# A two-block float32 model on one NeuronCore: order of the first up-projection stage's vector steps, and of the first pair of weight units

## The reference

```
xn = rms_norm(h, g_ffn) * (1 + sc2) + sh2
up = causal_dwconv(xn @ w_up, conv_ffn_w, conv_ffn_b)      # width 3, 2 * 2816 channels
val, gte = split(up, 2)
h = h + ga2 * ((silu(gte) * val) @ w_down)
```

## Time and profile before

| what | value |
|---|---|
| median of 3 runs | 1910.57 us (1907.24 to 1911.62) |
| the profiled execution's own time | 1908.22 us |
| its span, first to last instruction | 1906.4 us |
| PE busy | 1801.7 us, 95% |
| POOL busy | 1445.2 us, 76% |
| DVE busy | 1054.7 us, 55% |
| ACT busy | 532.1 us, 28% |
| mean granted TensorE clock | 0.980 |

### The profile page before, as it was taken

How to read it: one execution, slowest core, us unless ns; L and a number is a source line. 1 busy time by engine, 2 the same in 40 slices (tenths; PEclk the granted TensorE clock), 3 DMA queues, 4 the chain that set the end, 5 groups by cost and what they waited for, 6 DMA issues and landing times.

```text
span 1906.4 us, 33520 instructions
## 1 busy us (share of the span) xinstructions
PE 1801.7 (95%) x11324; PEld 1585.4 (83%) x11324; DVE 1054.7 (55%) x1674; ACT 532.1 (28%) x784; POOL 1445.2 (76%) x2245
## 2 busy tenths in 40 slices
PE   4999988999898999999899999999999999999997
PEld 2767765578698999888799999999999999999885
DVE  6548887745746666621375556656555555555101
ACT  3236662310221111110244434443443221111000
POOL 1768982469978888799677767767776889999885
PEclk8999997999999999999999999999999999999999
DMA  8332332334522222233222222222222223323332
GB/s 311 116 111 88 94 105 100 100 133 154 152 80 88 77 88 77 88 99 99 66 79 78 67 68 77 78 67 68 77 68 69 86 88 99 94 93 91 102 105 88
DMA packets 54299, 184.42 MB, mean 97 GB/s; under 512 B 6673, under 2 KB 7857, under 8 KB 54226
## 3 DMA queue, kind: packets, MB, share of 16 engines
q1 hardware_dynamic: 48690, 169.20, 28.5%
q10 hardware_dynamic: 5536, 14.16, 2.2%
HBM read 178.62 MB, written 4.72 MB: 96 GB/s over the span
## 4 chain that ended last, share of the span: by engine, by line
PE 55%; POOL 14%; issue 11%; DVE 7%; DVEq 5%; ACT 3%; DMA 3%; SPq 1%; POOLq 0%; ACTq 0%
PE gp L378 17%; PE gp L379 17%; PE gp L380 17%; POOL Wlo L369 9%; POOL Whi L366 3%; PE A L680 3%; DMA raw<-units 2%; DVEq L1395 2%; POOL probe L365 2%; DVEq L1446 2%; DVE ffn_act L1402 1%; DVE ffn_gate L1399 1%; DVE AClo L1379 1%; DVE ffn_gate L1397 1%; ACT ffn_val L953 1%
## 5 line engine op out<-in xcount | busy, mean ns | idle before, releaser
L369 POOL TENSOR_TENSOR Wlo<-raw,Whi 128x256 fp32r<-128x256 f32 x1120 | 961.3, 879 | 46.8
L378 PE MATMUL gp<-XNhi,Whi 128*128 128x264 f32 (+3 forms) x2736 | 845.3, 309 | 57.2 <-DVE XNlo L1072 23.8
L379 PE MATMUL gp<-XNlo,Whi 128*128 128x264 f32 (+3 forms) x2736 | 834.5, 305 | 0.0
L380 PE MATMUL gp<-XNhi,Wlo 128*128 128x264 f32 (+3 forms) x2736 | 831.7, 304 | 0.0
L378 PEld LDWEIGHTS gp<-XNhi,Whi 128*128 128x128 f32 x2736 | 517.3, 189 | 89.8 <-POOL Wlo L369 33.2
L379 PEld LDWEIGHTS gp<-XNlo,Whi 128*128 128x128 f32 x2736 | 517.4, 189 | 25.5 <-issue 2.2
L380 PEld LDWEIGHTS gp<-XNhi,Wlo 128*128 128x128 f32 x2736 | 516.6, 189 | 22.9
L365 POOL TENSOR_TENSOR probe<-raw 1x1 f32<-1x1 f32 x560 | 164.5, 294 | 393.2 <-PE gp L380 350.6
L366 POOL TENSOR_SCALAR Whi<-raw 128x512 fp32r<-128x512 f32 x560 | 344.3, 615 | 0.0
L378 PE MATMUL gp<-AChi,Whi 128*128 128x512 f32 x352 | 139.1, 395 | 1.2 <-DVE ZZ L1394 1.2
L379 PE MATMUL gp<-AClo,Whi 128*128 128x512 f32 x352 | 139.0, 395 | 0.0
(11 more groups left out here) (301 smaller groups left out, 2230.7 us busy)
## 6 DMA issues: line engine op xcount, KB each, us to landing
raw<-units SPq DMA_DIRECT2D x280, 512.0 KB, 3.5
AW<-ada SPq DMA_DIRECT2D x16, 512.0 KB, 9.1
AWL<-ada SPq DMA_DIRECT2D x16, 512.0 KB, 4.0
AWL<-ada ACTq DMA_DIRECT2D x16, 512.0 KB, 4.2
bias_rows<-RB ACTq DMA_DIRECT2D x1, 2560.0 KB, 16.4
H<-xT SPq DMA_DIRECT2D x1, 2048.0 KB, 8.9
BIAS<-bias_rows ACTq DMA_DIRECT2D x1, 2048.0 KB, 9.3
out<-H SPq DMA_DIRECT2D x8, 256.0 KB, 2.1
```

What stands on the lines that cost most here:

```text
L369: ins = pool.tensor_tensor(lo[:, c:c + UNIT // 4], src[:, c:c + UNIT // 4], hi[:, c:c + UNIT // 4].bitcast(F32), ALU.subtract)
L378: pe.matmul(dst, Whi[s][:, k, :], rhi, start=start, stop=False)
L379: pe.matmul(dst, Whi[s][:, k, :], rlo, start=False, stop=False)
L380: return pe.matmul(dst, Wlo[s][:, k, :], rhi, start=False, stop=stop)
```

## The change

In first_pair the second unit stands six steps behind the first one (lag = 6) and stats(m) is called at step 6. So PE does chunks 0 to 5 of the first unit, the statistics, chunks 6 and 7 of the first unit by turns with 0 and 1 of the second, and then the other six of the second. This holds for all three first pairs.

In the first up stage DVE's order is changed: the product and the split of a pair are issued inside the steps of the next pair, the product in the place where DVE waited for ACT's first tap of the value, the split where it waited for that of the gate. For this the value has two buffers; gate, silu and product keep one each. ACT may run one pair further ahead of act_done, whose count starts one higher. The loops are unrolled by two.

```diff
-            YV, YG, SL, AF = [sb(f"ffn_{n}", [P, S], frame=f) for n in ("val", "gate", "silu", "act")]
+            YV, YV1, YG, SL, AF = [sb(f"ffn_{n}", [P, S], frame=f) for n in ("val", "val1", "gate", "silu", "act")]
+            YVS = (YV, YV1)
...
-                lag = 1
+                lag = 6
                 for j in range(KC + lag):
-                    if j == KC // 2 and midway is not None:
+                    if j == lag and midway is not None:
                         midway()
...
-            all_units(*down(U_DN, G_DN, (act_done, 1)))
+            all_units(*down(U_DN, G_DN, (act_done, 2)))
...
-            with act.Fori(0, FC) as i:
-                for c, (y, first) in enumerate(((YV, yv_first), (YG, yg_first))):
-                    act.wait_ge(z_ready, i * 2 + c + 1)
-                    if c == 0:
-                        act.wait_ge(act_done, i + 1)
...
+            with act.Fori(0, FC // 2) as i:
+                for j in range(2):
+                    for c, (y, first) in enumerate(((YVS[j], yv_first), (YG, yg_first))):
+                        act.wait_ge(z_ready, i * 4 + (j * 2 + c + 1))
+                        if c == 0:
+                            act.wait_ge(act_done, i * 2 + j + 1)
...
+            dve.memset(probe[0:1, 22:23], 0.0).then_inc(act_done, 1)
...
-            with dve.Fori(0, FC) as i:
...
+            def product_up(i, j):
+                dve.wait_ge(silu_ready, i * 2 + j + 1)
+                dve.tensor_tensor(AF[:, :], SL[:, :], YVS[j][:, :], ALU.mult)
+                dve.drain()
+
+            def pair_up(i, j, before):
...
                     dve.drain().then_inc(z_ready, 1)
-                    dve.wait_ge(first, i + 1)
+                    if before is not None:
+                        if c == 0:
+                            product_up(*before)
+                        else:
+                            split_act(before[0] * 2 + before[1], act_done)
+                    dve.wait_ge(first, i * 2 + j + 1)
                     dve.scalar_tensor_tensor(y[:, :], ZZ[:, c, 1:1 + S], fv(4 * c + 1), y[:, :], ALU.mult, ALU.add)
...
-                dve.wait_ge(silu_ready, i + 1)
-                dve.tensor_tensor(AF[:, :], SL[:, :], YV[:, :], ALU.mult)
-                split_act(i, act_done)
+            pair_up(0, 0, None)
+            pair_up(0, 1, (0, 0))
+            with dve.Fori(1, FC // 2) as i:
+                pair_up(i, 0, (i - 1, 1))
+                pair_up(i, 1, (i, 0))
+            product_up(FC // 2 - 1, 1)
+            split_act(FC - 1, act_done)
```

More of the change, by code:

```diff
@@ L947, in _ @@
             act.preload_act_table(ACT.Silu)
-            with act.Fori(0, FC) as i:
-                for c, (y, first) in enumerate(((YV, yv_first), (YG, yg_first))):
-                    act.wait_ge(z_ready, i * 2 + c + 1)
-                    if c == 0:
-                        act.wait_ge(act_done, i + 1)
[L953 to L956, removed]
+            with act.Fori(0, FC // 2) as i:
[4 more added lines that the diff above has]
+                            act.wait_ge(act_done, i * 2 + j + 1)
+                        act.activation(y[:, :], ZZ[:, c, 2:2 + S], ACT.Identity, bias=BC[:, c:c + 1],
+                                       scale=V[:, bass.ds(VEC["ffn"] + i * 16 + (j * 8 + 4 * c + 2), 1)]).then_inc(first, 1)
+                    act.wait_ge(yg_ready, i * 2 + j + 1)
+                    act.activation(SL[:, :], YG[:, :], ACT.Silu).then_inc(silu_ready, 1)
             norm_stats(2)
@@ L1384, in _ @@
             dve.wait_ge(rstd_ready, 2)
-            with dve.Fori(0, FC) as i:
-                def fv(c):
[L1387 to L1391, removed]
+            b0 = region(S + 2)
+            def product_up(i, j):
[3 more added lines that the diff above has]
+            def pair_up(i, j, before):
+                def fv(c):
+                    return V[:, bass.ds(VEC["ffn"] + i * 16 + (j * 8 + c), 1)]
+                taps = TAPS[:, bass.ds(i * 2 + j, 1), :].rearrange("p a c -> p (a c)")
+                for c, (y, first) in enumerate(((YVS[j], yv_first), (YG, yg_first))):
+                    dve.wait_ge(unit_done, U_UP + i * 4 + (j * 2 + c + 1 + 2))
                     dve.scalar_tensor_tensor(BC[:, c:c + 1], gp[c][:, b0 + 1:b0 + 2], taps[:, c:c + 1], fv(4 * c + 3), ALU.mult, ALU.add)
```

## The result

The changed kernel runs at a median of 1885.4 us (1883.61 to 1887.6, four runs) against 1911.09 before; the ratio is 0.9861 with a 95% interval of 0.9827 to 0.9895. That is 1.4% faster; the forecast was 1883 us. The profiled execution took 1887.12 us with a span of 1885.3.

A forecast was written before the change was run, and what follows sets the result against it. DVE, with its waits for ACT, was taken to bound the first up stage. 23.8 + 6.3 - 2.4 = 27.7 us off the profiled 1908.22 gave 1880.5; with the median 2.35 us above that execution, 1883 was named, range 1874 to 1897.

The forecast's parts named there:

- the loop: First up stage: interleaving takes pairs from 12.645 to 11.55 us, POOL a little over PE's pace; 23.8 us gained.
- Rival 1: First up stage's loop: PE alone paces it, POOL's price 0.27 or less; total 1878.5 us; chance 0.2.
- rival 2: First up stage's loop: POOL bounds it at 11.8 to 12.35 us a pair; total 1888 to 1899 us; chance 0.22.
- Two of my signs: Loop: PE's waits are for L369 if POOL binds; DVE has no wait over 0.2 us before L1397.
- The price of POOL: Loop: each us of DVE's busy time slows POOL by 0.30 us, with DVE at 8.28 us a pair.
- the third rival: Loop: each us of DVE's two-input work costs POOL a full us; 14.9 us a pair, total 1952; chance 0.02.
- The first up pair: First up stage's first pair: no gap between matmuls, end 13.3 us after its start, 6.3 us gained.
- The first projection: First projection's first pair: late activations and a later clock rise lose 2.4 us, range 0 to 3.0.
- The second up stage's first pair: Second up stage: PE has no gap, so the edit is worth 0; about 1 us lost if XN came late.
- DVE's last chain: End of first up stage: last split moves to about 10 us after the last up unit; no cost was added.

The follow-up runs named there:

- e4: Changed kernel, but POOL makes only the first 256 columns of Wlo in each half in the first up stage's units; loop 237.4 us, median 1886.1 us.
- e1: Kernel before plus the interleaving of DVE's steps alone, lag 1 and statistics at step 4; 1893.0 us, ratio 0.9892.
- e8b: Changed kernel plus one DVE tensor_tensor per unit of the first up stage, first input from PSUM, second from SBUF; 1887.0 us, ratio 0.9874.
- e8a: Changed kernel plus one DVE tensor_tensor per unit of the first up stage, both inputs from SBUF; loop 261.3 us, median 1903.2 us.
- e3: Changed kernel with lag 1 in the first projection alone; 1882.9 us, ratio 0.9852.
- e9: The changed kernel run again, unaltered, for its profile; 1881.5 us, ratio 0.9845.

## Why the prediction was right, and where it was not

**The total** (1883, measured 1885.4) and the loop came out by the stated mechanism. The wait for L1394 is gone. POOL took its place: I put 11.55 us a pair for the loop, measured are 11.52; 23.8 us of gain against 24.3. e4 shows that it is POOL, e1 that the interleaving alone gives 21.9 us of it. That the loop is met so closely is in part luck. Where POOL sets the pace a pair takes 11.65 us, which over 20 pairs would have been 21.8 us of gain by my own sum; and I gave POOL no lead, which keeps the first eight pairs at 11.31. The two errors nearly cancel. Rival 1 was short by POOL's 4.5 us, rival 2 needed 11.8 us a pair. Two of my signs did not show: no wait of a matmul for L369 is listed in the loop (they are too short), and DVE still waits 0.38 us ahead of the first tap of the value, not under 0.2.

**The price of POOL** was 0.30 us per us of DVE, and the profile gives (2.916 - 2.26) / 1.987 us of DVE per half = 0.33; DVE's busy time per pair came out at 7.9 instead of 8.28 us, so the product is nearly the same. Its unit did not survive e8b. By the Trainium skill (SBUF — State Buffer, "Who interferes with whom") an instruction of VectorE with at most one input from SBUF, outside its two-port modes, does not contend with GpSimd. e8b agrees: the loop took 241.4 us with such an instruction more in each unit, 241.9 without. The same section of the Trainium skill calls the ports that the two share an exclusive lock. e8a shows what that came to here: 0.43 us on POOL for each added instruction, which itself took 1.22 us, so the third rival's price of a full us per us was not seen.

**The first up pair** was to end 13.3 us after its start and did after 13.43; the gain is 6.2 us against 6.3. The root was ready early enough, and gp[0] too.

**The first projection** was the step that was sized too low: 2.4 us, with 3.0 as the upper end; the mean of the runs is 3.0 (21.2 against 18.2). The cause is the one given, a clock that rises later. In the changed kernel PE had six chunks with pauses of some 0.6 us between them while the activations came, then ran at the lower clock to 58.45 us, 5.7 us after its last pause, where I had put 4.7 (54.3 to 59.0 us):

```profile
52.74 0.79 PE L379 MATMUL gp<-XNhi,Whi 128*128 128x512 f32 x1 [0.59 <-DVE XNlo L1074]
...
58.03 0.63 PE L379 MATMUL gp<-XNhi,Whi 128*128 128x512 f32 x1
58.45 0.43 PE L380 MATMUL gp<-XNlo,Whi 128*128 128x512 f32 x1
58.72 0.39 PE L381 MATMUL gp<-XNhi,Wlo 128*128 128x512 f32 x1
```

P0 follows that moment. With lag 6 the matmuls became faster 14.6 (e4) to 17.1 us (changed) after the first one, and P0 took 20.6 to 21.8 us (in the mean 15.9 and 21.2; my 59.0 us was 15.6 after it); with lag 1, 9.4 (e1) to 12.3 us (e3) after it, and P0 took 17.5 to 18.8. I missed that POOL, released earlier, now works beside DVE's last activations: they are there 13.6 us after the first matmul in all six kernels with lag 6, and after 12.2 to 12.7 us in those with lag 1. PE had to wait for neither of the last two chunks.

**The second up stage's first pair** was put at 0; matmuls 9216 to 9408, which hold it, take 29.8 us with lag 6 in all kernels that have it and 29.5 with lag 1: 0.3 us lost.

**What I left out.** First, a POOL that bounds the loop has nothing in hand when the down stage begins. In the first hundred matmuls of that stage the changed kernel, e1, e3, e8b and e9 lose 0.6 us against before, e8a 0.9, and e4, with POOL's work cut, nothing. I had only asked whether DVE's last chain was in time for the down stage (it was). The rest of the 1.4 us by which the stretch behind is longer (141.1 against 139.7) falls at its other end, where PE, after a wait of 5.6 us for activations, runs at the lower clock for a stretch that differs between profiles. Second, the places where the clock falls outside the stage: the recurrence stage took 491.5 to 500.6 us, and five such places, of 1.5 us each, are most of the difference of 9. Added up for the profiled execution: -30.5 in the stage, +3.6 in P0 (this run's) and -2.0 since its activations came earlier, +1.4 behind the stage, and the remaining 6.4 us in stretches that the change does not touch, of which four more places of low clock (at 123, 345, 1410 and 1461 us, 1.5 us each) are the most.

## What to carry to other kernels

When an engine's wait for a helper is filled with the work of the pair before, ask at once who shares a resource with the work that now runs without pause. Here POOL was 15% idle, and one look at how its instructions lengthen beside DVE's put the new bound within 0.1 us a pair (11.55 against 11.65). Ask also how far ahead the helper is when the loop begins: here that was worth 2.4 us. Price such contention by kind of instruction: in this loop one with two inputs in SBUF cost the neighbour 0.43 us, one with an input from PSUM nothing; so look for the first kind. Taking a cast from SBUF to SBUF away from DVE helped too: one fewer per pair took 4 x 0.041 = 0.16 us off POOL's pair, all effects together, and 3.8 us off the stage. And a change of a shared helper, like the lag here, is to be priced at each place that calls it: with weights late a long lag pays, with activations late it costs.

Where stages outside the change differ by several us between runs of one kernel, compare the stage that was changed by the starts of its own first and last matmul; here that was good to 0.2 us (255.3 and 255.5), while the spans differed by 6.6.

## What the runs showed of the hardware

- PE's clock fell to its lower level in the recurrence stage at 1410.3 us, shortly after a single wait of 1.05 us (1.3 us between the starts of two matmuls, 1407.3 to 1408.6). In e9 the same wait, 1403.7 to 1405.0 us, left it up. e1 and e4 have four such places 68 us apart, in four passes of that stage's loop in a row, e8b five, the kernel before none. Each costs some 1.5 us.
- POOL's one-input instruction on 512 columns (Whi) took 607 to 619 ns beside all of DVE's work, nearly without exception, while its two-input instruction (Wlo) ranged from 725 to 1257 ns, and the one-element probe just ahead of Whi from 182 to 638. That is a matter of order and not of Whi's kind. The one exception between 600 and 750 us in the changed kernel is the one time that a DVE instruction with two inputs from SBUF had begun before it (in e8a and e9 it is so once each in the loop, with 1.06 us):

```profile
611.97 0.69 DVE L1392 TENSOR_TENSOR ffn_act<-ffn_silu,ffn_val 128x512 f32<-128x512 f32 x1
612.08 1.05 POOL L367 TENSOR_SCALAR Whi<-raw 128x512 fp32r<-128x512 f32 x1
```

  Elsewhere it is DVE that begins second: its taps and subtractions that begin over 0.4 us before the end of Whi take 0.97 to 1.03 us, where a tap can take 0.75.
